# Two-layer trunk on one core: the down projection in pairs of column blocks with seven block products in five groups of 22, and the gate's silu behind the first group of a chunk

## The reference

```python
x = x + jnp.concatenate([mix, mem_out], axis=-1) @ w_o[i]
gate, up = _split(rms_norm(x, norm_ffn[i]) @ w_gate_up[i], (D_FF, D_FF))
x = x + (jax.nn.silu(gate) * up) @ w_down[i]
```

## Time and profile before

| what | us |
|---|---|
| median of three executions | 2177.11 (2175.9 to 2177.83) |
| the profiled execution's own time | 2178.24 |
| its span, first to last instruction | 2176.4 |
| PE busy, in all | 2158.2 (99% of the span) |
| DVE busy, in all | 1555.4 (71%) |
| ACT busy, in all | 1095.3 (50%) |
| SP's queue waiting for DVE's `w_lo` (L1074), in all | 1181.6, 548 times |

### The profile page before, as it was taken

How to read it: one execution, slowest core, us unless ns; L and a number is a source line. 1 busy time by engine, 2 the same in 40 slices (tenths; PEclk the granted TensorE clock), 3 DMA queues, 4 the chain that set the end, 5 groups by cost and what they waited for, 6 DMA issues and landing times.

```text
span 2176.4 us, 29853 instructions
## 1 busy us (share of the span) xinstructions
PE 2158.2 (99%) x10052; PEld 1784.3 (82%) x10052; DVE 1555.4 (71%) x1937; ACT 1095.3 (50%) x1414; POOL 58.4 (3%) x99
## 2 busy tenths in 40 slices
PE   8999999999999999999999999999999999999999
PEld 6888888888888888888888888888878888888887
DVE  6657766888888885555566767677888888874443
ACT  7755654545555554444444444454454545544332
POOL 2101100000000000000100000000000000000000
PEclk9999999999999999999999999999999999999999
DMA  8765466667666666666555656566676666666664
GB/s 313 233 194 155 138 211 204 202 194 222 202 206 214 214 217 199 205 205 202 177 172 164 202 158 191 172 206 209 195 221 203 205 208 217 201 219 218 202 203 133
DMA packets 244569, 435.57 MB, mean 200 GB/s; under 512 B 23040, under 2 KB 43648, under 8 KB 244480
## 3 DMA queue, kind: packets, MB, share of 16 engines
q1 hardware_dynamic: 243392, 432.31, 63.7%
q10 hardware_dynamic: 1088, 2.10, 0.2%
HBM read 411.25 MB, written 2.10 MB: 190 GB/s over the span
## 4 chain that ended last, share of the span: by engine, by line
PE 70%; DVE 11%; issue 7%; SPq 6%; DMA 4%; ACT 2%; DVEq 1%; ACTq 0%
PE unit_bank L1801 52%; SPq L408 5%; PE mix_bank L1853 4%; PE mix_bank L1801 4%; DMA raw<-in_w_gate_up 4%; PE unit_bank L1853 3%; DVE w_lo L1074 3%; PE unit_bank L1813 1%; PE mix_bank L1813 1%; PE mix_bank L1871 1%; DVE sums L1096 1%; ACT w_hi L615 1%; PE mix_bank L2001 1%; DVE up_ff L1574 1%; DVE act_ff L1598 1%
## 5 line engine op out<-in xcount | busy, mean ns | idle before, releaser
L1074 DVE TENSOR_TENSOR w_lo<-raw,w_hi 128x1024 fp32r<-128x1024 f32 x687 | 828.8, 1220 | 472.8 <-ACT w_hi L615 450.7
L615 ACT ACTIVATE w_hi<-raw 128x1024 fp32r<-128x1024 f32 x687 | 719.0, 1057 | 603.4 <-PE unit_bank L1801 381.9
L1801 PE MATMUL unit_bank<-w_hi,gT_hi 128*128 128x512 f32 x704 | 217.1, 389 | 1.3 <-issue 1.3
L1801 PE MATMUL unit_bank<-w_lo,gT_hi 128*128 128x512 f32 x704 | 216.9, 389 | 0.0
L1801 PE MATMUL unit_bank<-w_hi,gT_lo 128*128 128x512 f32 x704 | 216.8, 389 | 0.0
L1801 PE MATMUL unit_bank<-w_hi,hT_hi 128*128 128x512 f32 (+1 forms) x576 | 181.2, 396 | 0.0
L1801 PE MATMUL unit_bank<-w_hi,hT_lo 128*128 128x512 f32 (+1 forms) x576 | 176.2, 387 | 0.0
L1801 PE MATMUL unit_bank<-w_lo,hT_hi 128*128 128x512 f32 (+1 forms) x576 | 175.9, 387 | 0.0
L1801 PEld LDWEIGHTS unit_bank<-w_hi,gT_hi 128*128 128x128 f32 x704 | 132.0, 188 | 29.4 <-issue 2.0
L1801 PEld LDWEIGHTS unit_bank<-w_lo,gT_hi 128*128 128x128 f32 x704 | 132.2, 188 | 27.5
L1801 PEld LDWEIGHTS unit_bank<-w_hi,gT_lo 128*128 128x128 f32 x704 | 132.2, 188 | 27.4
(11 more groups left out here) (348 smaller groups left out, 3113.9 us busy)
## 6 DMA issues: line engine op xcount, KB each, us to landing
raw<-in_w_gate_up SPq DMA_DIRECT2D x352, 512.0 KB, 4.2
raw<-in_w_down SPq DMA_DIRECT2D x176, 512.0 KB, 4.6
raw<-in_w_in_b SPq DMA_DIRECT2D x104, 512.0 KB, 4.0
raw<-in_w_o SPq DMA_DIRECT2D x64, 512.0 KB, 4.4
raw<-in_w_in_a SPq DMA_DIRECT2D x40, 512.0 KB, 3.9
moved<-turned SPq DMA_DIRECT2D x528, 32.0 KB, 2.6
raw<-in_w_mem_kv SPq DMA_DIRECT2D x31, 512.0 KB, 5.6
tanh_ff<-act_ff SPq DMA_DIRECT2D x112, 32.0 KB, 3.3
```

The lines of the kernel that those rows point to most:

```text
L615: act.activation(w_hi[:, s, :, :], raw[:, s, :, :], ACT.Copy).then_inc(sems["hi_ready"], 1)
L1074: dve.tensor_tensor(w_lo[:, s, :, :], raw[:, s, :, :], w_hi[:, s, :, :].bitcast(F32), ALU.subtract).then_inc(sems["lo_ready"], 1)
L1801: ins = pe.matmul(all_banks[2 * pair + tile][:, 0:cols], stationary[part][:, kt + j, tile * P:(tile + 1) * P], b[:, s, j, 0:cols], start=o ...
```

## The change

1. **Down projection.** It now takes two column blocks at a time (a pair, p = 0 and 1), so that a group is two row blocks by two column blocks. A pair has 22 groups, 44 pieces, and uses the chunk's eight banks. The groups 5, 8, 11, 13 and 15 (`DOWN_SEVEN`) get the seven products and `split_seven`. The last six groups run all of one side, then all of the other (`DOWN_SIDES`).
2. **Forms.** For each of the five groups DVE makes combinations of the stationary blocks (`down_form`, five instructions), ACT their high parts (`form_hi`, two), DVE their low parts (`down_form_lo`, two). In pair 0 `down_form` stands at the piece numbers 1, 9, 15, 20 and 24 (`FORM_STEPS`), `form_hi` one and `down_form_lo` two later. Pair 1 uses the same forms.
3. **Results.** `down_shared` (eight DVE instructions) at piece 33 and `down_own` add the banks to x.
4. **In the chunks** `gate_silu` on DVE moves from i = 1 to i = 3. ACT's tanh stays at i = 1.
5. In layer 0 one of the four transposes of x, with its 16 transfers, moves into the first unit of layer 1, and another to i = 8 of pair 1.

```diff
+DOWN_SEVEN = (5, 8, 11, 13, 15)
+FORM_STEPS = (1, 9, 15, 20, 24)
+DOWN_QUADS = FT // 2
+DOWN_SIDES = 6
...
@@ ACT
+                def form_hi(n):
+                    act.wait_ge(sems["form_ready"], t.next("form_ready"))
+                    act.activation(down_forms[0][:, n, :, :], down_work[:, 4:7, :], ACT.Copy)
+                    act.activation(gT[0][:, 2 * DOWN_SEVEN[n], P:2 * P], down_work[:, 7, :], ACT.Copy).then_inc(sems["hi_block"], 1)
...
@@ DVE, chunks
                     for i in chunk_pieces():
-                        if i == 1:
+                        if i == 3:
                             gate_silu()
...
@@ DVE, down
+            def down_pieces(last=False):
+
+                for i in range(DOWN_PIECES):
+                    yield i
+                    q, side = DOWN_ORDER[(i + LEAD) % DOWN_PIECES]
+                    if last and i + LEAD >= DOWN_PIECES:
+                        pass
+                    elif q not in DOWN_SEVEN:
+                        split()
+                    elif side == 0:
+                        split_seven(down_sums)
+                    t.move("at")
...
+                def down_form(n):
+
+                    kt, parts = 2 * DOWN_SEVEN[n], [down_work[:, m, :] for m in range(8)]
+                    hi, lo = (g[:, kt:kt + 2, :].rearrange("p k n -> p (k n)").bitcast(F32) for g in gT)
+                    dve.tensor_tensor(down_work[:, 0:4, :].rearrange("p k n -> p (k n)"), hi, lo, ALU.add).then_inc(sems["dve_chain"], 1)
+                    dve.wait_ge(sems["dve_chain"], t.next("dve_chain"))
+                    dve.tensor_tensor(parts[4], parts[1], parts[3], ALU.subtract).then_inc(sems["dve_chain"], 1)
+                    dve.tensor_tensor(parts[7], parts[1], parts[0], ALU.subtract)
+                    dve.wait_ge(sems["dve_chain"], t.next("dve_chain"))
+                    dve.tensor_tensor(parts[5], parts[0], parts[4], ALU.subtract).then_inc(sems["dve_chain"], 1)
+                    dve.wait_ge(sems["dve_chain"], t.next("dve_chain"))
+                    dve.tensor_tensor(parts[6], parts[2], parts[5], ALU.subtract).then_inc(sems["form_ready"], 1)
...
+                for p, (own, shared) in enumerate(chunk_banks):
+                    for i in down_pieces(layer == 1 and p == 1):
+                        if p == 0 and i == 3:
                             gate_silu()
-                        if c == 0 and i == 5:
+                        if p == 0 and i in FORM_STEPS:
+                            down_form(FORM_STEPS.index(i))
+                        if p == 0 and i - 2 in FORM_STEPS:
+                            down_form_lo(FORM_STEPS.index(i - 2))
+                        if p == 0 and i == 5:
                             times_up()
-                        if c == 0 and i == 12:
+                        if p == 0 and i == 14:
                             moved_block(gT, FT - 4, "gT_ready")
...
+                        if layer == 0 and p == 1 and i == 8:
+                            turn_added(1)
+                        if i == SHARED_STEP + 1:
+                            down_shared(p, shared)
+                        if i == LEFT_STEP:
+                            down_own(p, 0, own)
...
@@ PE
+            def down_products(p, own, shared):
...
+                for q, side in DOWN_ORDER:
...
+                    if q not in DOWN_SEVEN:
+                        plain_piece(gT, 2 * q, side, own, q == 0, q == DOWN_QUADS - 1)
+                    elif side == 0:
+                        n = DOWN_SEVEN.index(q)
+                        if p == 0:
+                            pe.wait_ge(sems["down_form_ready"], t.next("down_form_ready"))
+                        seven_products(gT, 2 * q, down_forms, n, down_sums, own, shared, n == 0, n == len(DOWN_SEVEN) - 1,
+                                       evicted if p == 0 else block_added)
```

More of the change, by code:

```diff
@@ L27 @@
+from collections import namedtuple
 from contextlib import ExitStack, contextmanager
@@ L495, in projection_ffn @@
                 wd = w_down[layer, :, :]
-                for c in range(BLOCKS):
-                    unit(wd, c * COLS, FF_KTS, between=moves({(11 if c == 0 else 8) + n: (4 * n, 4 * n + 4) for n in range(4)}) if c == 0 or layer == 0 else None)
+                down_turns = [{11 + n: (4 * n, 4 * n + 4) for n in range(4)}, {}]
+                if layer == 0:
+                    down_turns[1] = {first + n: (4 * n, 4 * n + 4) for first in (2, 15) for n in range(4)}
+                for p in range(2):
+                    for n, (q, side) in enumerate(DOWN_ORDER):
+                        piece(wd, 2 * q, (2 * p + side) * COLS)
+                        moves(down_turns[p])(n)
             wa = w_in_a[0, :, :]
@@ L506, in _ @@
             wb = w_in_b[0, :, :]
-            unit(wb, 4 * TOKEN_WIDTH)
+            unit(wb, 4 * TOKEN_WIDTH, between=moves({1 + n: (4 * n, 4 * n + 4) for n in range(4)}))
             in_group = {16 + n: (4 * n, 4 * n + 4, 1) for n in range(4)}
@@ L975, in projection_ffn @@
+                        if i == SHARED_STEP:
+                            act.wait_ge(sems["piece_used"], t.value("at"))
+                            act.activation(down_two[:, 0, :], shared[0][:, :], ACT.Copy).then_inc(sems["first_copied"], 1)
+                        if layer == 1 and i == LEFT_STEP + 2:
+                            store(2 * p)
                     if layer == 0:
-                        x_sums((pair, other)[c % 2], c)
+                        added_sums(2 * p)
+                        added_sums(2 * p + 1)
@@ L977, in projection_ffn @@
                     else:
-                        store((pair, other)[c % 2], c)
+                        store(2 * p + 1)
                 if layer == 1:
@@ L1119, in chunk_pieces, with down_pieces @@
                     elif ahead % 2 == 0:
-                        split_seven()
+                        split_seven(chunk_sums)
+                    t.move("at")
+            def down_pieces(last=False):
+                for i in range(DOWN_PIECES):
+                    yield i
+                    q, side = DOWN_ORDER[(i + LEAD) % DOWN_PIECES]
+                    if last and i + LEAD >= DOWN_PIECES:
+                        pass
+                    elif q not in DOWN_SEVEN:
+                        split()
+                    elif side == 0:
+                        split_seven(down_sums)
                     t.move("at")
@@ new lines, in projection_ffn @@
+                for p, (own, shared) in enumerate(chunk_banks):
+                    for i in down_pieces(layer == 1 and p == 1):
+                        if p == 0 and i == 3:
+                            gate_silu()
+                        if p == 0 and i in FORM_STEPS:
[3 more added lines that the diff above has]
+                        if p == 0 and i == 5:
@@ L1674, in slots @@
+                        if layer == 0 and p == 1 and i == 8:
[4 more added lines that the diff above has]
+                            down_own(p, 0, own)
+                        if layer == 0 and i == LEFT_STEP + 1:
+                            turn_added(2 * p)
+                    down_own(p, 1, own)
             def slots(n):
@@ L1814, in product, with seven_products @@
                 return ins
-            def seven_products(n, own, shared):
+            def seven_products(x, kt, forms, n, sums, own, shared, first, last, shared_ready):
                 s = slot[0] % RING
```

177 lines of the change are left out of this document (115 added, 62 removed).

## The result

| | before | changed |
|---|---|---|
| median, us | 2177.47 (2175.9 to 2178.12, 4 runs) | 2221.51 (2217.69 to 2224.63, 4 runs) |
| ratio, 95% interval | | 1.0203 (1.0185 to 1.022) |
| span of the profiled execution, us | 2176.4 | 2219.6 |

The kernel became 44 us slower. The forecast was 29 us slower (2206.5), and the range ended at 2217. The direction was right, and 15 us were not in the sum.

What follows compares the result with a forecast made beforehand. PE bounds the down projection, a closed DVE, SP, DMA and ACT ring the chunk loop. Span 2176.4 - 13.6 + 1.4 + 22 + 19 + 0.6 = 2205.8, so median 2206.5 us; range 2184 to 2217.

Steps and rivals of the forecast that it cites:

- Removed matmuls: Down projection: 60 matmuls fewer at 0.227 us each, 13.6 us less on PE, all of which counts.
- Bounds of groups: Down projection: 20 new bounds of groups at about 0.07 us each add 1.4 us.
- Silu: Chunk loops: silu behind the first group lengthens each of 20 chunks by 1.1 us, +22 us, bounds 0 and 27.
- the ring: Chunk loop: a closed ring through DVE, SP, DMA and ACT, 42.6 us without slack, sets the chunk's length; PE follows.
- two PE gaps a chunk: Sign in the chunk loop: two PE gaps per chunk instead of one, the new one 0.7 us before piece 6.
- Forms: Down projection, pair 0: forms behind groups of seven stall PE, 9.6 us a layer, +19 us in all, bounds 0 and 24.
- Pair 1 almost without any: Sign in the down projection: PE gaps fall in pair 0 before pieces 12, 18, 24 and 28, pair 1 having almost none.
- these transposes: Layer 0, pair 1: the transposes at i = 8 stand behind group 5 and cost 0.6 us, once.
- the ring had no slack: Answers a rival for the chunk loop: the ring has slack, silu costs nothing, down terms stand, 2184.5 us; 12%.
- the forms did not hide: Answers a rival for the down projection: PE's lead at groups hides the forms, silu costs 22, 2187 us; 8%.
- the lateness of DVE and ACT did reach PE: Answers a rival for the whole kernel: PE alone counts, DVE's and ACT's lateness never reaches it, 2165 or 2157 us; 11%.

Runs made afterwards that it cites:

- Silu late: The kernel before with the chunks' silu at i = 5, behind pieces 6 and 7 and ahead of `times_up`: 2202.73 us, ratio 1.0109.
- transfers spread: The kernel before with the chunk's 16 transfers four each behind pieces 11 to 14 instead of 6, 6 and 4 behind 11 to 13: 2167.33 us, 0.9975.
- half loads: The changed kernel with forms at 1, 6, 11, 16, 19 and each weight load of a group of seven halved to 256 KB: 2195.5 us, ratio 1.0079.
- loads first: The changed kernel with silu at i = 1, groups 5, 8, 11, 14, 17, forms apart, `moved_block` earlier, pair 1's transposes and transfers later: 2174.15 us, 1.0007.
- silu back: The changed kernel with the chunks' silu back at i = 1, the down projection staying changed: 2199.51 us, ratio 1.0094 to the kernel before.
- both: The "loads first" kernel with the chunk's 16 transfers four each behind pieces 11 to 14: 2168.75 us, ratio 0.996 to the kernel before.

## Why the prediction missed, by its own steps

- **Removed matmuls, 13.6 us: right.** The plain matmul is still 0.227. **Bounds of groups, 1.4:** 3.6 measured, as what is left of the 37 us when every stall and the clock are taken out. Most restarts have a second small gap of 0.11 behind them.
- **Silu, 22 us: right.** 20.2 in the loops, 21.4 when done alone; a chunk of 43.75 us against 43.9. "Silu late" and "transfers spread" show the ring from two more sides. Wrong was "two PE gaps a chunk": the old one went as the new one came, since the chunk has one ring and PE waits for it where it first meets it. The Trainium skill ("DMA: Bandwidth & Descriptors", Anatomy of one DMA) made this term near 0 by its 3.2 us for 512 KB. The section is on DMAs that GpSimd issues, and these are issued by SyncE. The trace does not agree with the 3.2 for them: 4.1 us is the median.
- **Forms, 19.2 us: right in sum, not in each, and the sum in part by luck.** The plain pieces' stalls are 16.6; the waits for group sums in pair 0, for which the prediction had 0.8 a layer, bring it to 20.0. Before pieces 12, 18, 24 it was 1.1, 2.3 and 2.9 against 0.9, 2.1 and 2.9. Before piece 28 it was 1.2 and 2.7 against 2.9: in layer 0 the slow matmuls behind piece 24 had made PE 1.6 us later. `down_form` holds DVE 1.7 us (878.39 to 880.13), as estimated.
- **"Pair 1 almost without any": wrong.** This is the step that failed: 7.9 us where the sum had nothing. The prediction followed the ring of the chunks and laid none for the down projection, where groups of seven stand two apart. Both loads of a group are issued 0.4 us apart there (the sum `down_all` frees both slots), and the second lands after 4.7 to 5.5. The ring of a group is then 11.3 to 12.1 us against 10.2 of PE's work between groups 11, 13 and 15. Even with the 4.20 us of a load of gate and up it would be 12.06 - 5.52 + 4.20 = 10.7, an estimate, so the missing ring was the error, and the longer landing made it larger. It cost 5.1 us in both layers, with group 11's wait, and "half loads" shows the cause. The other 2.8 us are at group 8 of layer 0, where the transposes' 16 transfers stand among its loads on SP; "loads first" moved them and that wait went. The prediction had these transposes as 0.6 us of DVE's work alone. That waits for sums lay behind the forms' too is why taking the forms away gave only 14.
- **The clock: left out.** 4.7 us behind three of the long form stalls, of which some 2.5 came back as shorter waits. The sum had the stalls, and at their ends the old speed. The 0.426 us of a matmul there is what the Trainium skill states for 1.2 GHz ("TensorE: Matmul & The Clock Gate", Back-to-back issue gap: the columns over 1.2 GHz, 0.427); the trace agrees. At full clock its 0.216 stays below the 0.227 of the rows.

Together: -13.6 matmuls, +3.6 bounds, +20.2 silu, +20.0 pair 0, +0.6 the transpose in pair 1, +7.9 loads in pair 1, +4.7 clock is 43.4, against 2219.6 - 2176.4 = 43.2. The forecast had 29.4. The 14 us between them are loads 7.9, clock 4.7, bounds 2.2 and pair 0 1.0, less 1.8 for silu; the fifteenth is in the step from span to median, 0.7 in the forecast and 1.9 measured. The rivals fell: the ring had no slack, the forms did not hide, and the lateness of DVE and ACT did reach PE.

## What to carry to other kernels

Where a ring of few slots feeds PE, take every ring's length (issue, landing with all loads that are in flight then, split, sums) and lay it against PE's work between two uses; fewer matmuls make that work shorter and can turn a hidden ring into the bound, so a shorter product pays only where it is far enough from the next. Small transfers on the queue that also issues the loads count by their issue time, and where they stand matters: with their number unchanged it was worth 5.6 us here. A stall of over 2 us may cost more than its length, since PE may come out of it at the lower clock.

## What the runs showed of the hardware

- A 512 KB load took 4.1 us (median) for gate and up and 4.7 for down. Of two issued 0.4 us apart in pair 1 the first took 4.0 and 3.8 us, the second 5.52 and 4.74; the longest of all took 7.2. 256 KB took 3.2. The Trainium skill ("DMA: Bandwidth & Descriptors", Anatomy of one DMA) has 2.0 us plus bytes over 436 GB/s for DMAs that GpSimd issues; by it 256 KB are 2.6 us and 512 KB 3.2, estimates that these loads, issued by SyncE, exceed by 0.6 to 1.5. Why they take longer, and why the loads of down take longer than those of gate and up, stays open.
- A 32 KB transfer keeps SP's queue for 0.6 us (four in 2.41). The Trainium skill ("DMA: Bandwidth & Descriptors", Issuing engines are not separate DMA queues) calls the time to initiate a DMA "usually small relative to the DMA itself"; here it is 0.6 us beside 2.5 to landing, and 16 of them hold the queue for 9.6 us, longer than two loads take to land.
- The clock fell behind stalls of 2.3, 2.9 and 2.7 us and did not behind others of 2.4 and 2.9 (2018.55 and 2038.36) nor behind any of 1.6 or less in the down projections; in "silu back" it fell behind the stalls of 2.3 and 2.9 at these same two places; and the stall at the start of layer 1, 2.7 us in "loads first" and 2.8 in "both", had no slow matmul behind it in the one and 7 in the other. The length of a stall alone doesn't decide it. What else does was not tried.
